# Parameter rows on ScalarE's queue, a first weight unit in four pieces, and identity products on TensorE in the start of a hybrid encoder layer with 32 experts

## What is computed

```python
def layer(x, ...):
    z = rms_norm(x, norm1_g) @ w_in            # 1024 -> 5120, split into six parts
    xc, new_buf = causal_conv(xa, conv_buf, conv_w, conv_b)
    h, h_last = rg_lru(xc, h0, ...)            # recurrent branch
    v = layer_norm(gelu(v)); vmix = chunk_spatial_mix(v)
    merged = sigmoid(gate_a) * (h * gelu(ga)) @ w_proj_a + sigmoid(gate_b) * (gelu(u) * vmix) @ w_proj_b
    x = x + merged @ w_out
    return x + moe(rms_norm(x, norm2_g))       # top 4 of 32 experts
```

## Time and profile before

| | |
|---|---|
| three runs | 1233.7, 1235.17, 1238.72 us; median 1235.17 |
| span of the profiled execution | 1237.9 us, from the first to the last instruction |
| TensorE busy | 1184.7 us, 96% |
| VectorE, ScalarE, GpSimd busy | 394.3, 224.0, 82.7 us |
| moved from and to memory | 443.69 MB, mean 358 GB/s |
| mean granted TensorE clock | 0.992 of 2.4 GHz |

### The profile page before, as it was taken

One profiled execution on the slowest core, in us unless ns is written; L12 is line 12 of the kernel. 1 busy time (PEld: TensorE's weight loads), 2 busy tenths in 40 slices (PEclk: granted clock), 3 DMA queues, 4 the chain that ended last, 5 costly groups with the idle time before them and its releaser, 6 DMA issues.

```text
span 1237.9 us, 16075 instructions
## 1 busy us (share of the span) xinstructions
PE 1184.7 (96%) x6459; PEld 679.0 (55%) x6459; DVE 394.3 (32%) x647; ACT 224.0 (18%) x383; POOL 82.7 (7%) x242
## 2 busy tenths in 40 slices
PE   6999999999999999899998999999999998999996
PEld 5999999986435353344434343535535353553542
DVE  4647586665334423021212111111212111221222
ACT  4543582233101010101101010101101010110111
POOL 3200000010201001101000010101011010100000
PEclk9999999999999999999999999999999999999999
DMA  7454326587999999999999999999999999999993
GB/s 227 133 159 134 102 86 211 191 341 290 425 426 429 427 429 424 426 427 426 427 428 426 429 422 422 408 383 428 428 426 429 427 427 427 428 428 429 425 424 153
DMA packets 51854, 443.69 MB, mean 358 GB/s; under 512 B 4956, under 2 KB 5052, under 8 KB 23040
## 3 DMA queue, kind: packets, MB, share of 16 engines
q1 hardware_dynamic: 50512, 439.43, 86.0%
q0 software_dynamic: 1264, 3.20, 1.1%
HBM read 440.63 MB, written 1.98 MB: 358 GB/s over the span
## 4 chain that ended last, share of the span: by engine, by line
PE 79%; DMA 17%; issue 2%; DVE 1%; SPq 1%; ACT 0%; POOLq 0%; POOL 0%; DVEq 0%; ACTq 0%
PE ps L1587 25%; PE ps L1650 19%; DMA wexp<-in_w_gate_up_dram 13%; PE ps L1500 8%; PE ps L1251 7%; PE ps L1252 7%; PE ps L1253 7%; DMA wexp<-in_w_down_dram 2%; PE ps L1516 1%; PE ps L1550 1%; PE ps L1517 1%; PE ps L1602 1%; PE ps L1351 1%; DMA raw<-in_w_in_dram 1%; PE ps L1508 1%
## 5 line engine op out<-in xcount | busy, mean ns | idle before, releaser
L1587 PE MATMUL ps<-wexp,xt 128*64 128x512 f32 (+1 forms) x2368 | 473.9, 600 | 24.7 <-DMA wexp<-in_w_gate_up_dram 18.7
L1587 PEld LDWEIGHTS ps<-wexp,xt 128*64 128x64 f32 (+1 forms) x2368 | 153.8, 132 | 315.4 <-issue 314.7
L1650 PE MATMUL ps<-wexp,act_t 128*64 128x512 f32 (+1 forms) x1184 | 230.5, 593 | 5.9 <-issue 3.2
L1650 PEld LDWEIGHTS ps<-wexp,act_t 128*64 128x64 f32 (+1 forms) x1184 | 86.9, 131 | 136.7 <-issue 136.6
L1166 DVE TENSOR_TENSOR y<-y,ps 128x1024 f32<-128x1024 f32 x51 | 60.7, 1218 | 217.2 <-PE ps L1517 215.2
L755 ACT ACTIVATE g<-g 128x512 f32<-128x512 f32 x33 | 20.8, 630 | 554.1 <-DVE g L1180 554.1
L1251 PE MATMUL ps<-act_h,split 128*128 128x384 f32 x352 | 117.9, 335 | 0.0
L1253 PE MATMUL ps<-act_h,split 128*128 128x384 f32 x352 | 117.6, 334 | 0.0
L1252 PE MATMUL ps<-act_l,split 128*128 128x384 f32 x352 | 117.6, 334 | 0.0
L1500 PEld LDWEIGHTS ps<-pick,xn 128*128 128x128 f32 x768 | 91.1, 196 | 14.8 <-issue 14.8
L1500 PE MATMUL ps<-pick,xn 128*128 128x128 f32 x768 | 94.1, 283 | 1.7 <-POOL pick L535 1.7
(11 more groups left out here) (307 smaller groups left out, 818.6 us busy)
## 6 DMA issues: line engine op xcount, KB each, us to landing
wexp<-in_w_gate_up_dram SPq DMA_DIRECT2D x106, 2048.0 KB, 22.3
wexp<-in_w_down_dram SPq DMA_DIRECT2D x52, 2048.0 KB, 23.4
wexp<-in_w_gate_up_dram SPq DMA_DIRECT2D x44, 1024.0 KB, 18.3
wexp<-in_w_down_dram SPq DMA_DIRECT2D x22, 1024.0 KB, 8.2
raw<-in_w_in_dram SPq DMA_DIRECT2D x20, 1024.0 KB, 5.1
raw<-in_w_proj_a_dram SPq DMA_DIRECT2D x4, 1024.0 KB, 5.6
raw<-in_w_out_dram SPq DMA_DIRECT2D x4, 1024.0 KB, 5.0
raw<-in_w_proj_b_dram SPq DMA_DIRECT2D x2, 1024.0 KB, 6.7
```

The source lines that it names most:

```text
L1587: i_ = pe.matmul(ps[s0:s0 + w, b, :], xt[:, k, s0:s0 + w], wexp[place(k, x) % RINGS][:, at_:at_ + UC], start=k == 0, stop=k == CB - 1)
L1650: i_ = pe.matmul(ps[s0:s0 + w, 6 + c, :], act_, wexp[place(CB + m, x) % RINGS][:, D * kk + UC * c:D * kk + UC * c + UC], start=k == 0, sto ...
```

## The change

The seven parameter loads are issued by ScalarE, ahead of everything else in its list. SP issues unit 0 right behind the input, as four loads of one block each with a semaphore of their own, then unit 1, then the state. ScalarE rounds unit 0 block by block, block j ahead of `act_h` 0, 2, 4 and 5; VectorE takes the low parts ahead of `act_l` 0, 3, 5 and 6. VectorE copies the turned rows before anything else, and TensorE turns them before any input. TensorE multiplies the identity matrix by itself 10 times ahead of the rows, 10 times behind them, twice ahead of tile 1 and 6 times ahead of the last block of tile 2; the results are not used.

```diff
         late_loaded, y_loaded, bias_loaded = sem("late_loaded"), sem("y_loaded"), sem("bias_loaded")
         fnb_loaded, n2p_loaded = sem("fnb_loaded"), sem("n2p_loaded")
         mix_landed = [sem(f"mix_landed{i}") for i in range(MIX_RING)]
+        first_landed, high_first = [sem(f"first_landed{j}") for j in range(KB - 1)] + [mix_landed[0]], sem("high_first")
         exp_landed = [sem(f"exp_landed{i}") for i in range(RINGS)]
         last_landed = [[sem(f"last_landed{k}{x}") for x in range(2)] for k in range(2)]
         last_gate_up = sem("last_gate_up")
...
             for t in range(2):
                 sp.dma_start(x_in[:, t, :], x_prompt[:, t * P:(t + 1) * P, :].rearrange("o p d -> (o p) d")).then_inc(x_loaded[t], 16)
             sp.dma_start(x_in[:, 2, :], x_sample.rearrange("b s d -> (b s) d")).then_inc(x_loaded[2], 16)
-            for r, a in ((G1_R, norm1_g), (CBIAS_R, conv_b), (BRG_R, b_rg), (BIG_R, b_ig), (LAM_R, lru_lambda), (N2_R, norm2_g)):
-                sp.dma_start(rows[r:r + CB, :], a.rearrange("o (c p) -> (o c) p", p=P)).then_inc(rows_loaded, 16)
-            sp.dma_start(rows[CONVW_R:N2_R, :], conv_w.rearrange("o k (c p) -> (o k c) p", p=P)).then_inc(rows_loaded, 16)
             def load_expert(n):
 
                 sp.dma_start(wexp[n][:], exp_one(n % 2, n // 2)).then_inc(exp_landed[n], 16)
...
             for n in range(MIX_U):
                 if n >= MIX_RING:
                     sp.wait_ge(low_done, n - MIX_RING + 1)
+                if n == 0:
+                    for j in range(KB):
+                        sp.dma_start(raw[:, 0, j], mix_unit(0)[:, j]).then_inc(first_landed[j], 16)
+                    continue
                 sp.dma_start(raw[:, n % MIX_RING], mix_unit(n)).then_inc(mix_landed[n % MIX_RING], 16)
-                if n == 0:
+                if n == 1:
                     sp.dma_start(state_in[0:24, :], state_conv.rearrange("o b k d -> (o b k) d")).then_inc(state_loaded, 16)
                     sp.dma_start(state_in[24:32, :], state_h.rearrange("o b d -> (o b) d")).then_inc(state_loaded, 16)
                 if n == PA_U:
...
                     act.wait_ge(unit_used, n - MIX_SPLIT + 1)
                 act.activation(split_h[:, n % MIX_SPLIT], raw[:, n % MIX_RING], ACT.Copy).then_inc(high_done, 1)
 
+            for r, a in ((G1_R, norm1_g), (CBIAS_R, conv_b), (BRG_R, b_rg), (BIG_R, b_ig), (LAM_R, lru_lambda), (N2_R, norm2_g)):
+                act.dma_start(rows[r:r + CB, :], a.rearrange("o (c p) -> (o c) p", p=P)).then_inc(rows_loaded, 16)
+            act.dma_start(rows[CONVW_R:N2_R, :], conv_w.rearrange("o k (c p) -> (o k c) p", p=P)).then_inc(rows_loaded, 16)
             act.preload_act_table(ACT.Sqrt)
             def square_input(t):
 
...
             square_input(2)
             root_input(1)
             root_input(2)
-            high(0)
+
+            def high_part(j):
+
+                act.wait_ge(first_landed[j], 16)
+                act.activation(split_h[:, 0, j], raw[:, 0, j], ACT.Copy).then_inc(high_first if j < KB - 1 else high_done, 1)
+
             act.wait_ge(rows_copied, 1)
             for c in range(CB):
+                for j in {0: (0,), 2: (1,), 4: (2,), 5: (3,)}.get(c, ()):
+                    high_part(j)
                 act.wait_ge(xs_turned, c + 1)
                 act.activation(act_h[:, c, :], ps[:, c, 0:T], ACT.Identity, scale=cols[:, G1_R + c:G1_R + c + 1]).then_inc(xn_high, 1)
             high(1)
...
                 dve.wait_ge(rstd_out, t + 1)
                 dve.tensor_scalar(scale[:, t, :], ident[:], st8[:, 8 + t:9 + t], None, ALU.mult).then_inc(scale_ready, 1)
 
+            dve.wait_ge(rows_turned, 1)
+            link(dve.tensor_copy(cols[:], ps[:, 7, T:T + N2_R]))
+            dve.tensor_copy(n2c, ps[:, 7, T + N2_R:T + ROWS]).then_inc(rows_copied, 1)
             dve.wait_ge(const_ready, 1)
             for t in range(TT):
                 dve.wait_ge(squared, t + 1)
                 link(dve.tensor_scalar(st8[:, 4 + t:5 + t], st8[:, t:t + 1], 1.0 / D, RMS_EPS, ALU.mult, ALU.add))
                 dve.reciprocal(st8[:, 4 + t:5 + t], st8[:, 4 + t:5 + t]).then_inc(rstd_in, 1)
                 token_scale(t)
-                if t == 1:
-                    dve.wait_ge(rows_turned, 1)
-                    link(dve.tensor_copy(cols[:], ps[:, 7, T:T + N2_R]))
-                    dve.tensor_copy(n2c, ps[:, 7, T + N2_R:T + ROWS]).then_inc(rows_copied, 1)
+
             def low_part(j):
 
-                dve.wait_ge(high_done, 1)
+                if j < KB - 1:
+                    dve.wait_ge(high_first, j + 1)
+                else:
+                    dve.wait_ge(high_done, 1)
                 dve.tensor_tensor(split_l[:, 0, j], raw[:, 0, j], split_h[:, 0, j].bitcast(F32),
                                   ALU.subtract).then_inc(low_first if j < KB - 1 else low_done, 1)
 
             for c in range(CB):
-                for j in {0: (0,), 3: (1, 2), 4: (3,)}.get(c, ()):
+                for j in {0: (0,), 3: (1,), 5: (2,), 6: (3,)}.get(c, ()):
                     low_part(j)
                 dve.wait_ge(xn_high, c + 1)
                 i_ = dve.scalar_tensor_tensor(out=act_l[:, c, :], in0=ps[:, c, 0:T], scalar=cols[:, G1_R + c:G1_R + c + 1],
...
                     if t == TT - 1:
                         i_.then_inc(xs_turned, 1)
 
-            turn_input(0, range(0, 7))
+            def spin(n, bank):
+
+                for _ in range(n):
+                    pe.matmul(ps[:, bank, T:T + P], ident[:], ident[:], start=True, stop=True)
+
+            spin(10, 6)
             pe.wait_ge(rows_loaded, 7 * 16)
             pe.transpose(ps[:, 7, T:T + ROWS], rows[:], ident[0:ROWS, 0:ROWS]).then_inc(rows_turned, 1)
-            turn_input(1, range(0, 7))
+            spin(10, 6)
+            turn_input(0, range(0, 7))
             pe.wait_ge(rows_copied, 1)
             turn_input(0, range(7, 8))
-            turn_input(1, range(7, 8))
-            turn_input(2, range(0, 8))
+            spin(2, 6)
+            turn_input(1, range(0, 8))
+            turn_input(2, range(0, 7))
+            spin(6, 7)
+            turn_input(2, range(7, 8))
 
             def channel_unit(slot, k_blocks, bank, act_hl, start, stop, ready=None, before=None):
 
```

## The result

| | before | after |
|---|---|---|
| median of 14 runs each | 1236.06 us | 1239.62 us |
| lowest to highest | 1233.7 to 1238.73 | 1237.85 to 1241.5 |
| span of the profiled execution | 1237.9 | 1237.0 |

The ratio is 1.0031, 95% interval 1.0022 to 1.0039: the changed kernel is slower by 2.7 to 4.8 us (by medians 3.6), where 2.3 faster was forecast. The difference is smaller than the 0.5% that the prediction took for the least that can be told from no change, but the interval leaves no doubt of the direction, and the time lies outside the stated range. The two profiled spans say the opposite, 0.9 us faster. That contradiction is taken up with the experiments.

The account below looks back on a forecast made before the run. Mixer bound by TensorE, experts by transfers, both released by the start. 0.75 us at the first product plus 1.65 by the clock, less 0.1 for the scale's hand-over, gave 2.3: 1235.17 to 1232.9 us; range 1229.3 to 1237.2.

Parts of the forecast that it names:

- The landing of the rows: Parameter loads on ScalarE's queue: last row landed at 6.0 us, between bounds of 5.6 and 9.2.
- The pace of the identity products: Head of TensorE's list: 0.44 us per product until 5.0, then 0.235; first ten end at 5.5.
- 16.3: Forecast start in us of TensorE's first product with weights, with the clock up, against 17.03 before.
- the late clock: Rival: identity products slow until 8.4, first product at 17.6, price 1.3 us, time 1234.2; chance 0.17.
- The base: Profiled start of before: slow clock in the first 36 matmuls lost 1.65 us; times started from median 1235.17.
- the fall is not in every execution: Rival: the clock stays up through TensorE's 2.40 us idleness in other executions; gain only 0.75, time 1234.4; chance 0.13.
- the mark: Turn of the state on TensorE (line 1295), behind the first 36 matmuls: forecast near 24.6 us instead of 27.05.
- I count no earlier landing: Unit 0's load: issued at 2.22 instead of 4.67, yet its last piece still lands at 13.7 us.
- late rows, slower than before: Rival at TensorE's wait for `rows_loaded`: landing beyond 6.0 passes through, deciding from 8.3; 1236.1 at landing 9.2; chance 0.10.
- a time moved by more than the mark: Sign of being wrong: measured time shifts more than the turn of the state behind the first 36 matmuls.
- rows turned after 8.3: Sign of being wrong: TensorE turns the parameter rows later than 8.3 us, where near 6.0 was expected.
- unit 2's slack: Mixer: unit 2's low part ready ahead of TensorE's need; slack falls from 3.3 to 1.8 us and still covers.

Follow-up runs that it names:

- no second ten: The kernel after without the ten identity products behind the rows, the other 18 kept: 1240.63 us, ratio 1.0032 against before.
- the further profiles: The kernel before, unedited, profiled three more times: spans 1234.2, 1231.8 and 1234.2 us.
- the rows first: The kernel after with the parameter loads on SP's queue, ahead of the input: 1236.59 us, ratio 1.0003 against before.
- ten at the head, both loads: The kernel before with parameter loads on ScalarE, unit 0 in four pieces, and ten identity products heading TensorE's list: 1234.15 us, ratio 0.9986.
- twelve at the head: The kernel before with unit 0 in four pieces and twelve identity products heading TensorE's list, rows on SP's queue: 1233.95 us, ratio 0.9977.

## Why the prediction was wrong

*The landing of the rows*, "6.0", is the step that failed first. The bounds were 5.6 and 9.2 and I took a value near the lower one, by the small pieces of `ws_raw` (2.3 us), which travel when little else does. Measured, by the turn of the rows: 8.02 and 8.47 in the kernel after, 8.79 to 9.16 in the kernels made from it that do not issue the rows ahead of the input. The landing is set by what is in flight. By the Trainium skill, "Trainium Kernel Development and Optimization", section "Key Constraints", all queues share the 16 engines; the runs agree (8.93 with the rows on SP's queue, 8.02 to 9.16 on ScalarE's), and the row to go by was the one I used as the bound, the sample tile's 5.9.

*The pace of the identity products* failed second: "slow until 5.0". The first ten were to end at 5.5; they did so in one kernel (no second ten, 3.92 us), ran slow to their end, at about 6.2, in four of the other six profiles with ten at the head (4.63 us), and the twelve took 5.44. Then came a wait of 2 us, and ten more at 0.44 us, 4.35 us in place of 2.35. The two errors add 2.0 + 2.0 to my 16.3, and the first product started at 20.53 (20.29 by the timeline): the sum was right in its form. The rival "the late clock", given 0.17, had this place, a second ten at the slow pace, at 1.3 us; it was 2.0, and it came together with the late rows, which no case of the forecast had. In the second profile of after the clock had come up and fell again behind that wait, at about 9.8, in the midst of the second ten (a view of one microsecond counts six to seven records at the slow pace, eleven to twelve at the fast one):

```profile
8.60:9.60 1.00, 1.00 (x10) 1.00 (x11) 0.65 (x4) 0.05 (x1) 0.00 (x0) 1.00 1.07 412
...
10.60:11.60 1.00, 1.00 (x6) 1.00 (x6) 0.62 (x3) 0.28 (x3) 0.99 (x2) 0.50 1.05 395
```

With the rows back on SP the granted clock fell in the wait itself, which ends at 8.93:

```profile
7.60:8.60 1.00, 0.00 (x0) 0.00 (x0) 0.00 (x0) 0.00 (x0) 0.00 (x0) 1.00 0.90 256
8.60:9.60 1.00, 0.67 (x3) 0.68 (x4) 0.23 (x1) 0.00 (x0) 0.00 (x0) 0.55 0.95 328
```

So the late rows also took away what the first ten had bought.

*The base.* 1.65 of the 2.3 us were a slow stretch that the first profile had and the three further ones do not: the rival "the fall is not in every execution", given 0.13, is what the further profiles show. The Trainium skill, "TensorE: Matmul & The Clock Gate", section "What's actually happening", has it that the count of slow products differs between runs; four profiles of before agree: one with the fall, three without, and the 34 records of the turning behind the rows took 4.05, 4.40, 5.33 and 4.01 us, as the slow pace lasted longer or shorter. I had also written that nothing in the forecast depended on what made that execution long. It did: the same unlucky start that was to be mended made 2.9 of the 3.5 us by which its span, 1237.9, lies above the 1234.4 that the median less 1.7 gives. The median it started from, 1235.17 of three runs, was itself 0.9 us under that of fourteen. At the mark: 24.6 was forecast and 28.4 measured (mean), 3.8 us by the rows and the pace, and the base was 24.2 and not 27.05, another 2.9.

*"I count no earlier landing"* was wrong to the other side: unit 0 was whole by 10.44, at least 1.7 us ahead of the further profiles of before. It could not help, as it was off the path.

*The rival "late rows, slower than before"* was the right mechanism, in the right place, and had 0.10. Its point of decision, 8.3 us, was reckoned from the unlucky profile, and with the pace of "slow until 5.0". Against the further profiles, whose first product starts at 15.5 to 15.9, the forecast's own 16.3 is already late; each microsecond of the landing beyond 6.0 only adds. Of the signs of being wrong, "a time moved by more than the mark" was there at once (3.6 against 1.7), and "rows turned after 8.3" in every kernel made from it but the one with the rows first.

*Right*: that a shift goes through mixer and experts whole; that unit 2's slack covers (no wait of TensorE for it in any run); that VectorE's and ScalarE's interleaving keeps up with TensorE; that the issues on ScalarE's queue cost nothing on the path of this kernel (0.28 to 0.60 us each, square at 4.90), since both engines wait for the rows anyway.

## What to carry to other kernels

A wait for a small transfer, put at the head of two engines' lists, is as long as the traffic beside it makes the transfer, not as long as its size does; put the work that is ready first, and let the small rows be turned when they have surely landed. Identity products belong where the engine would be idle anyway, close ahead of real work: there they moved the mark by 2 us, while on the path the last eight only cost, and where a wait of 1.8 to 3.3 us stood behind the first ten, their gain was gone by the time that the real work began. And take several profiles of one kernel before a gain of 2 us is built on one of them.

## What the runs showed that was not expected

Four profiles of one kernel differed by 3.2 us in the start alone (23.89 to 27.05), and the stretch from the mixer's end to the end of the span took 950.4 to 954.7 us over all seventeen profiles, whatever the kernel. Two spans of the profiler can thus have the opposite order of the medians. Ten identity products in front, then 1.3 us of waiting, left the clock up (ten at the head, both loads: tile 0's seven blocks in 1.83 us); the same ten, then a wait of 3.3 us and one of 1.4, did not (no second ten: eight blocks in 3.79).

Time less span, near 1.7 us in almost every run, reached 2.6 to 2.8 in single runs of three kernels (no second ten, twelve at the head, ten at the head) and in none of before on the same chip. Why is not known. By the medians of their spans these three shift by +3.9, -2.7 and -2.3 us, closer to their marks (+4.1, -2.5, -2.5) than by the medians of their times.
